# Order and queues of the first loads, and eight neighbouring rows of gate and up per partition

## What is computed

```python
c_act = jax.nn.silu(c)
for l in range(DEPTH):
    mod = c_act @ ada_w[l] + ada_b[l]
    sh1, sc1, g1, sh2, sc2, g2 = [t[:, None, :] for t in jnp.split(mod, 6, axis=-1)]

    h = rms_norm(x, norm_mix_w[l]) * (1.0 + sc1) + sh1
    proj = h @ w_in[l]
    ...
    x = x + g1 * (merged @ w_out[l])

    h2 = rms_norm(x, norm_ffn_w[l]) * (1.0 + sc2) + sh2
    x = x + g2 * grouped_moe(h2, router_w, router_bias, w_gate[l], w_up[l], w_down[l])
```

## Time and profile before

| | us |
|---|---|
| median of 3 runs | 1703.74 |
| the runs | 1700.13 to 1704.67 |
| profiled execution | 1704.2 |
| its span | 1702.6 |
| TensorE busy | 1488.8 (87%) |
| VectorE busy | 642.8 (38%) |
| ScalarE busy | 324.3 (19%) |
| DMA, mean over the span | 225 GB/s |

### The profile page before, as it was taken

One profiled execution on the slowest core, in us unless ns is written; L12 is line 12 of the kernel. 1 busy time (PEld: TensorE's weight loads), 2 busy tenths in 40 slices (PEclk: granted clock), 3 DMA queues, 4 the chain that ended last, 5 costly groups with the idle time before them and its releaser, 6 DMA issues.

```text
span 1702.6 us, 18332 instructions
## 1 busy us (share of the span) xinstructions
PE 1488.8 (87%) x5723; PEld 666.5 (39%) x5724; DVE 642.8 (38%) x1573; ACT 324.3 (19%) x825; POOL 126.8 (7%) x165
## 2 busy tenths in 40 slices
PE   2999999989992899989759999999999558999993
PEld 0544445544441333323234444454444223333331
DVE  1346434557524122112144554365763411121223
ACT  3223421100001112112143242111000111121220
POOL 1100000001102000000031000000110110000002
PEclk9999999999996799999979999999999869999997
DMA  8961112367706699999766012126773479996895
GB/s 265 386 249 49 51 50 84 114 249 294 279 18 247 183 347 392 379 389 390 267 236 221 1 50 86 62 99 232 262 253 142 152 271 381 392 387 230 304 383 181
DMA packets 140466, 383.34 MB, mean 225 GB/s; under 512 B 18760, under 2 KB 20984, under 8 KB 140408
## 3 DMA queue, kind: packets, MB, share of 16 engines
q1 hardware_dynamic: 107224, 273.04, 44.0%
q0 software_dynamic: 21664, 83.89, 13.1%
q10 hardware_dynamic: 11520, 25.70, 4.9%
HBM read 346.95 MB, written 35.65 MB: 225 GB/s over the span
## 4 chain that ended last, share of the span: by engine, by line
PE 74%; DMA 10%; DVE 5%; issue 5%; ACT 2%; POOL 1%; SPq 1%; POOLq 0%; ACTq 0%; DVEq 0%
PE bank L1041 23%; PE bank L1260 17%; PE bank L1030 11%; PE bank L1272 8%; PE bank L1208 5%; DMA weight_ring<-in_w_up_dram 4%; DMA regA<-in_w_up_dram 2%; PE bank L1252 1%; DMA h_features<-in_ada_w_dram 1%; DMA expert_rows<-merged_features 1%; PE bank L1108 1%; SPq L391 1%; PE bank L1266 1%; PE bank L1097 1%; POOL expert_rows L636 1%
## 5 line engine op out<-in xcount | busy, mean ns | idle before, releaser
L1041 PE MATMUL bank<-h_features,weight_ring 128*128 128x512 f32 x768 | 345.2, 603 | 2.0 <-ACT regB L756 2.0
L1260 PE MATMUL bank<-weight_ring,merged_features 128*64 128x512 f32 x960 | 224.9, 623 | 14.6 <-DMA weight_ring<-in_w_up_dram 7.5
L1041 PEld LDWEIGHTS bank<-h_features,weight_ring 128*128 128x128 f32 x768 | 146.7, 194 | 183.8 <-issue 183.5
L1030 PE MATMUL bank<-weight_ring,h_features 128*128 128x512 f32 (+1 forms) x512 | 196.3, 541 | 0.7 <-DVE h_features L1403 0.7
L1821 DVE TENSOR_TENSOR merged_features<-bank,merged_features 64x512 f32<-64x512 f32 x44 | 30.5, 693 | 364.2 <-ACT merged_features L890 364.2
L1030 PEld LDWEIGHTS bank<-weight_ring,h_features 128*128 128x128 f32 x512 | 95.9, 190 | 94.8 <-issue 90.7
L1260 PE MATMUL bank<-h_features,merged_features 128*64 128x512 f32 x256 | 116.7, 610 | 18.0 <-DMA regA<-in_w_up_dram 17.0
L1260 PEld LDWEIGHTS bank<-weight_ring,merged_features 128*64 128x64 f32 x960 | 72.1, 143 | 143.6 <-issue 138.9
L1272 PE MATMUL bank<-weight_ring,merged_features 128*64 128x512 f32 x528 | 120.6, 598 | 1.6 <-DVE merged_features L1808 1.6
L1260 PE MATMUL bank<-regA,merged_features 128*64 128x512 f32 x256 | 117.2, 612 | 0.0
L1208 PE MATMUL bank<-weight_ring,merged_features 128*128 128x512 f32 x256 | 114.3, 608 | 3.0 <-POOL merged_features L614 3.0
(11 more groups left out here) (319 smaller groups left out, 1456.6 us busy)
## 6 DMA issues: line engine op xcount, KB each, us to landing
weight_ring<-in_w_gate_dram SPq DMA_DIRECT2D x22, 2048.0 KB, 12.7
weight_ring<-in_w_up_dram SPq DMA_DIRECT2D x22, 2048.0 KB, 18.9
weight_ring<-in_w_down_dram POOLq DMA_DIRECT2D x22, 2048.0 KB, 16.7
weight_ring<-in_w_in_dram SPq DMA_DIRECT2D x18, 2048.0 KB, 17.7
x_tokens<-in_ada_w_dram SPq DMA_DIRECT2D x14, 2048.0 KB, 8.0
h_features<-in_w_gate_dram SPq DMA_DIRECT2D x10, 2048.0 KB, 11.4
regA<-in_w_up_dram SPq DMA_DIRECT2D x10, 2048.0 KB, 20.2
regA<-in_ada_w_dram SPq DMA_DIRECT2D x8, 2048.0 KB, 8.0
```

What stands on the lines that cost most here:

```text
L1030: ins = te.matmul(bank[:, 0:w], hT[:, k, P * i:P * i + P], wv[:, k, :], start=(k == 0), stop=(k == KD - 1))
L1041: ins = te.matmul(bank[:, :], wv[:, k, c0:c0 + P], rhs[:, k, :], start=(k == 0), stop=(k == kn - 1))
L1260: ins = te.matmul(ps[3][64 * part:64 * part + 64, :], xT[:, k, :], w[:, k, :], start=(k == 0), stop=(k == KD - 1))
```

## The change

SyncE's first issues are `crow`, the four pieces, q and kv. ScalarE issues the positions, x, the router bias, the router matrix (one transfer now) and `params(0)` ahead of its own first instruction. `params` has 16 transfers for 18, and the waits on `params_in` count so. Three of them write columns directly into `pc`; `prm` has 68 rows instead of 128, and the memset of its last rows is gone.

Features of the second half are kept eight to a partition: partition p holds features 8p to 8p+7. `whole_rows` reads gate and up with 8 neighbouring rows, 16 KB, per partition; the permuting copy reads every eighth value; `row_column_sums` sums pieces 6 to 9 by eight matmuls of 64 columns for four of 128, and `mod_chunk` copies 64 x 8 values for 128 x 4.

```diff
-        def of_pairs(w, l, e):
-
-            return w.rearrange("l e (m p r) f -> (l e) p m (r f)", p=P, r=2)[bass.ds(l * E + e, 1)].rearrange("a p m n -> p (a m) n")
...
+        def whole_rows(w, l, e, k):
+
+            return w.rearrange("l e (p k) f -> (l e) p (k f)", k=k)[bass.ds(l * E + e, 1)].rearrange("a p n -> p (a n)")
...
+            with nc.allow_non_contiguous_dma(reason="gate columns, biases and columns of parameters"):
+                rows(pc[:, 72:80], lay(norm_ffn_w, l).rearrange("a (p k) -> (a p) k", k=KD))
+                rows(pc[:, 80:88], lay(ada_b, l)[:, 3 * D:4 * D].rearrange("a (p k) -> (a p) k", k=KD))
+                rows(pc[:, 88:96], lay(ada_b, l)[:, 4 * D:5 * D].rearrange("a (p k) -> (a p) k", k=KD))
...
-            load_head(0)
-            sp.wait_ge(zeroed, 2)
-            for r in range(2):
-                sp.dma_start(rwz[:, r:KD:2, 0:E], router_w.rearrange("(m p r) e -> p m r e", p=P, r=2)[:, :, r, :]).then_inc(const_in, 16)
-            params(0)
-            sp.dma_start(xs[:, :, :], x.rearrange("a (i p) d -> p (a i) d", p=P)).then_inc(x_in, 16)
-            for j in range(1, HEAD_ADA):
+            for j in range(HEAD_ADA):
                 load_head(j)
...
-                    params(nxt)
+                    params(sp, nxt)
...
+            act.dma_start(xs[:, :, :], x.rearrange("a (i p) d -> p (a i) d", p=P)).then_inc(x_in, 16)
+            act.dma_start(rbias[:, :], router_bias.rearrange("(a e) -> a e", a=1).to_broadcast([P, E])).then_inc(const_in, 16)
+            act.wait_ge(zeroed, 1)
+            act.dma_start(rwz[:, :, 0:E], router_w.rearrange("(p k) e -> p k e", p=P)).then_inc(const_in, 16)
+            params(act, 0)
             act.wait_ge(dve_const, 1)
...
-                wait_head(pe, params_in, t, 18 * 16, 18 * 16)
-                te.transpose(ps[2][:, 0:P], prm[:, :], ident[:, :]).then_inc(param_cols, 1)
+                wait_head(pe, params_in, t, 16 * 16, 16 * 16)
+                te.transpose(ps[2][:, 0:68], prm, ident[0:68, 0:68]).then_inc(param_cols, 1)
...
+            def row_column_sums(bank, half, rows):
+
+                for k in range(KD):
+                    ins = te.matmul(bank[64 * half:64 * half + 64, k:k + 1], rows.rearrange("t (p k) -> t k p", k=KD)[:, k, :],
+                                    ones[:, 0:1], start=True, stop=True)
...
-                        link(ve.tensor_copy(modc[:, 4 * j:4 * j + 4], bank[:, 0:4]))
+                        r, c0 = 64 * (j % 2), KD * (j // 2)
+                        link(ve.tensor_copy(modc[r:r + 64, c0:c0 + KD], bank[r:r + 64, 0:KD]))
...
-                    ve.tensor_scalar(xn[:, i, :].rearrange("t (m r p) -> t m r p", r=2, p=P), xs[:, i, :].rearrange("t (m p r) -> t m r p", p=P, r=2),
+                    ve.tensor_scalar(xn[:, i, :].rearrange("t (k p) -> t k p", p=P), xs[:, i, :].rearrange("t (p k) -> t k p", k=KD),
```

More of the change, by code:

```diff
@@ L560, in _ @@
             pool.wait_ge(zeroed, 1)
-            po.memset(prm[96:P, :], 0.0).then_inc(zeroed, 1)
-            pool.wait_ge(zeroed, 2)
             po.memset(cz[:, :, :], 0.0)
@@ L663, in _ @@
             ac = nc.scalar
+            with nc.allow_non_contiguous_dma(reason="positions by token"):
+                act.dma_start(rt[:, 0:NT].bitcast(I32), positions.rearrange("a (i p) -> p (a i)", p=P)).then_inc(const_in, 16)
+            act.dma_start(xs[:, :, :], x.rearrange("a (i p) d -> p (a i) d", p=P)).then_inc(x_in, 16)
[3 more added lines that the diff above has]
+            params(act, 0)
             act.wait_ge(dve_const, 1)
@@ L950, in _ @@
             pe.wait_ge(dve_const, 3)
-            def paired_sums(bank, rows):
-                for q in range(4):
-                    ins = te.matmul(bank[:, q:q + 1], paired(rows, q), ones[:, 0:1], start=True, stop=True)
-                return ins
             def column_sums(bank, rows):
@@ L1381, in head_cols @@
                 wait_head(dve, param_cols, t, 1, 1)
[L1382 removed]
+                hlink(ve.tensor_copy(pc[:, 0:68], ps[2][:, 0:68]))
             def head_mod(raw):
[L1386 removed]
+                hlink(ve.tensor_tensor(modc[:, 0:16], raw, pc[:, 52:68], ALU.add))
                 hlink(ve.scalar_tensor_tensor(A1[:, :], modc[:, 8:16], 1.0, pc[:, 0:8], ALU.add, ALU.mult))
```

71 lines of the change are left out of this document (29 added, 42 removed).

## The result

The changed kernel takes 1732.29 us (median of 4 runs, 1725.31 to 1732.99) where the kernel before, on the same chip, takes 1703.57: a ratio of 1.0163, 95% interval 1.0133 to 1.0193. It is slower, as forecast, but by 28.7 us where 9.2 had been worked out, and it lies above the range. The profiled execution is the shortest of the four, 1725.3 us (span 1723.7, granted clock 0.946); the other three have a clock of 0.940 or 0.941 and take 7 us more. So the trace can explain 21 us; the rest goes with a lower clock, and no trace shows where it falls.

What follows compares the result with a forecast made beforehand. TensorE bounds the kernel (74% of the chain; transfers 10%). Head 6.2, weights -1, column sums 3 and copy 1 sum to +9.2 us: 1713 us, own range 1703 to 1724, 8-in-10 range 1696 to 1724.

Steps and rivals of the forecast that it cites:

- Direction and head: Slower overall; at the head, parameters behind the stream delay the first q product to 57.3 us, +6.2 us.
- One to one: Head: queues alternate by packets, so each small packet waits for one large packet, 98 ns beside 2 KB packets.
- Rival 1: Head: small packets pass beside the stream without costing a turn, q at 43.3 us; 1696 us, chance 0.18.
- Gate and up: Expert weights: 16 KB packets load faster but starve down, turning layer 1's up wait into a down wait; together -1 us.
- rival 4: Expert weights: gate and up rows are split again into 4 KB packets; 1714 us, chance within the forecast's 0.62.
- rival 3: Expert weights: 16 KB packets are slow, 273 GB/s; 1765 us, chance 0.05.
- the share: Experts: turns by packets leave down's queue 21% of about 410 GB/s, 85 GB/s; layer 1 +2.5 us.
- the forecast's -3.5: Layer 0's experts: faster weight loading with the deferred bytes, no wait for down taken, -3.5 us.
- the rate's gain: Gate and up: 16 KB packets move 430 GB/s against 410, 5% on two thirds of the bytes; 3.1 us in layer 0.
- A 64-column load has 137 ns for 196: Mixer column sums: eight 64-column loads for four of 128, sum 1.4 us, up to 2.0; +3 us over both layers.
- VectorE's copy: Permuting copy ahead of the second half: reading every eighth value takes 1.3 us for 754 ns; +1 us.

Runs made afterwards that it cites:

- e8: Changed kernel with the two gate-column transfers on a semaphore of their own, waited for only ahead of the gates' product: 1725.24 us, ratio 1.0106.
- e9: Changed kernel with VectorE writing partial sums of pieces 6 to 9 in TensorE's order, so weight loads read neighbouring values: 1725.61 us, ratio 1.0148.
- e12: Kernel before with the four 128-column matmuls of each column sum of pieces 6 to 9 run twice: 1714.69 us, ratio 1.0073.
- e4: Changed kernel with the eight 64-column matmuls of each column sum of pieces 6 to 9 run twice: 1746.07 us, ratio 1.0262.
- e1: Changed kernel with the head's issue order of the kernel before, SyncE issuing all: 1713.84 us, ratio 1.0084.
- e3: Changed kernel with gate and up matrices loaded in 4 KB packets instead of 16 KB: 1728.30 us, ratio 1.0142.
- e5: Changed kernel with the down matrices also loaded in packets of up to 16 KB: 1741.01 us, ratio 1.0202.
- e6: e1 with the down matrices also loaded in packets of up to 16 KB: 1732.22 us, ratio 1.0147.

## Why the prediction was wrong

*Direction and head: right.* The constants were seen at 22.15 us (20), ScalarE's first square at 29.19 (27.0), the parameters at 41.9 (41.6), q at 58.13 (57.3). One to one, taken from 22 small packets among 67, is 1969 to 2147 in the changed kernel, and e8 priced 128 small packets per engine at 12.5 us. Rival 1 is excluded. That the parameters came within 0.3 us is in part luck: the constants were 2.1 us late, and from there to the parameters it took 19.75 us where 21.6 had been reckoned (with 145 ns for each 4 KB packet, which no row shows; x had been reckoned at 160 + 83). The first parameter transfer held ScalarE for 7.24 us in its issue, which wasn't foreseen; that it cost nothing more isn't shown.

*Gate and up: mechanism right, size wrong.* The wait for up did turn into one for down, and the packets were whole (8250 packets of 8 KB or more on the page, 8192 forecast), so rival 4 is out, and rival 3 with it (the stream kept its 354 to 400 GB/s). But layer 1's wait was 17.0 us for the 9 forecast. The step that failed was the share: "21% of about 410 GB/s, 85 GB/s" counted two queues. There is a third, ScalarE's with the token rows, which took 108 of the 376 packets; down got 67 GB/s. In layer 0, where I took no wait for down, there were 16.3 us of it. There it only replaced 17.7 us for up, and the first expert products ran 2.5 us shorter (8.59 and 8.78 us for 10.03 and 9.83), so the -4.4 us look like the forecast's -3.5 but aren't the rate's gain.

*The rate's gain: not there.* I gave 16 KB packets 5% more rate. Where TensorE waits for supply, in 740:770 and 1430:1460 us, the changed kernel has 400 and 386 GB/s, the kernel before 394 in both.

*TensorE: the step that failed most.* "A 64-column load has 137 ns for 196" was a row of loads that read neighbouring values. The new loads read every eighth and took 217 ns; the sum takes 2.08 us, 1.08 more, a little over the upper end that I had given (2.0 us). That makes 6.5 us on the chain for the 3 taken. And the sum left out what can follow a longer stretch of such small matmuls: the granted clock falls to half, and eight products of 3.6 us take 5.2 to 5.4. In the profiled execution four sums were followed by that, three of them on the chain, 5.0 us; e9 (shorter sums, none), e12 (longer sums in the kernel before, 11 us) and e4 tie it to the sums' length. Where the clock falls changes from run to run: layer 1's mixer took 470 us in the changed kernel and in e1, and 476 to 478 in e3, e5, e6 and e8. The number of sums with slow products behind them is nearly the same in all six, three or four of eight, so it doesn't make that difference: it matters whether they are on the chain, and the clock also falls elsewhere in the mixer (0.59 in 1068:1080 in e8, 0.86 at the same place of the changed kernel, 1072:1084). That such falls are the 7 us between the profiled execution and the median, and e1's spread of 21 us, is likely; no trace of a longer run of the changed kernel itself shows it.

*VectorE's copy*: 1.15 us for 0.75, TensorE waited 5.0 us for 4.6 in each layer: +0.4 each, where +1 had been taken for both.

In the profiled execution the two mixers and the routing lost 10.5 us: 6.5 for the sums' length, 0.8 for the copy and 5.0 for the clock behind three sums make 12.3; elsewhere, mostly by the clock, layer 0 lost 2.4 us more and layer 1 gained 4.3 (1.7 of them behind the wait shown above). With the head's 7 and the experts' 5.5 that is 23, less 1.9 behind the experts, for which no run gives a cause. The range's upper end, 1724, has each term near its own end, but none of them had the clock.

## What to carry to other kernels

Queues that share DMA engines take turns by packets: before giving one stream larger packets, count the packet sizes of all queues that run beside it, since the one with the smallest packets loses bytes, and what it feeds is the next wait. Small transfers that are waited for belong ahead of the stream, or on a semaphore that isn't waited for early. And small matmuls between large ones can cost more than their length: look at the granted clock behind them, and take a price only from a row with the same access pattern.

## What the runs showed of the hardware

- One to one between queues by packets held from 16 byte packets beside 2 KB (1969 to 2147) to 4 KB beside 16 KB (131 to 137, with a third queue at 108). 16 KB packets brought no more rate than 4 KB ones where TensorE waits (400 and 386 GB/s for 394 in both stretches before).
- A weight load of TensorE took 138 ns for 64 neighbouring columns, 217 for 64 that are every eighth value, 192 for 128 neighbouring and 196 for 128 that are every second.
- VectorE's accumulation over 512 values took 752 ns, and 1111 when it read its sum and wrote it at every 64th value; its copy of 1024 values 754 ns reading every second, 1152 reading every eighth.
- The granted clock was 1.00 (2.4 GHz) in the mixer around column sums of 1.0 us, and 0.50 (1.2 GHz) for some 3 us (292:295) behind sums of 2.08 us, in 23 of 48 cases: products mostly at 5.2 to 5.4 us for 3.6. Behind a wait of TensorE of 3.77 us it was 0.57 (1203:1206 in the kernel before).
